# Router matmuls by depth half for both token halves, and a routing with fewer dependent VectorE steps

## The reference, cut to what matters

```python
h = rmsnorm(x, norm2_g[l]) * (1.0 + sc2) + sh2
scores = sigmoid(t @ w_router)                     # t: 256 x 1024, w_router: 1024 x 16
biased = (scores + router_bias).reshape(-1, 4, 4)
group_score = top_k(biased, 2)[0].sum(-1)
gmask = one_hot(top_k(group_score, 1))
masked = where(gmask, biased, -inf).reshape(-1, 16)
_, eidx = top_k(masked, 2)
w = sel / sel.sum(-1)                              # sel: the scores at eidx
y = sum over e of combine[:, e] * ((silu(t @ w_gate[e]) * (t @ w_up[e])) @ w_down[e])
```

## Time and profile before

| | us |
|---|---|
| median of 3 runs (1921.39, 1922.25, 1922.89) | 1922.25 |
| the profiled execution's own time | 1920.49 |
| its span, first to last instruction | 1918.9 |
| PE busy | 1844.8 (96%) |
| DVE busy | 761.5 (40%) |
| ACT busy | 660.6 (34%) |
| mean granted clock of TensorE | 0.991 |

### The profile page before, as it was taken

The page is one execution under the profiler, slowest core; times in us unless marked ns, Lnnn a source line. Parts: engine busy times, 40 slices in busy tenths (PEclk is TensorE's granted clock), DMA queues, the critical chain, the costliest instruction groups (busy, mean ns, idle before and its releaser), DMA issues.

```text
span 1918.9 us, 28438 instructions
## 1 busy us (share of the span) xinstructions
PE 1844.8 (96%) x11852; PEld 1309.1 (68%) x11852; DVE 761.5 (40%) x1285; ACT 660.6 (34%) x1064; POOL 65.3 (3%) x128
## 2 busy tenths in 40 slices
PE   5999999989999999999999999999999999899998
PEld 3888785323335888784333336676799989679998
DVE  4593553000004683652000004222455566656554
ACT  2325441111114325532111122141244546645443
POOL 0000001100001000001100010000000000000000
PEclk9999999999999999999999999999999999999999
DMA  9769865999976675865999957879954433434440
GB/s 380 299 264 383 344 244 218 426 428 427 428 305 268 246 287 220 317 263 233 427 427 427 414 202 296 353 294 418 392 201 175 175 132 118 161 139 176 175 175 22
DMA packets 52754, 540.88 MB, mean 282 GB/s; under 512 B 6768, under 2 KB 11248, under 8 KB 21680
## 3 DMA queue, kind: packets, MB, share of 16 engines
q1 hardware_dynamic: 42800, 505.66, 65.3%
q0 software_dynamic: 9856, 33.82, 4.6%
HBM read 589.53 MB, written 28.84 MB: 322 GB/s over the span
## 4 chain that ended last, share of the span: by engine, by line
PE 79%; DMA 8%; DVE 7%; DVEq 2%; issue 2%; ACT 1%; SPq 1%; POOL 0%; POOLq 0%; ACTq 0%
PE bank L1356 14%; PE bank L990 11%; PE bank L991 11%; PE bank L992 11%; PE bank L1381 6%; PE bank L1027 6%; DMA ring<-in_w_up 5%; PE bank L1036 3%; PE bank L1559 3%; PE bank L1160 2%; PE bank L1486 1%; PE bank L1507 1%; SPq L837 1%; DMA ring<-in_lru_w_out 1%; PE bank L1334 1%
## 5 line engine op out<-in xcount | busy, mean ns | idle before, releaser
L990 PE MATMUL bank<-split_x,split_w 128*128 128x256 f32 x1024 | 290.7, 284 | 2.3 <-DVE split_w L2790 2.3
L992 PE MATMUL bank<-split_x,split_w 128*128 128x256 f32 x1024 | 290.4, 284 | 0.0
L991 PE MATMUL bank<-split_x,split_w 128*128 128x256 f32 x1024 | 290.4, 284 | 0.0
L2672 DVE TENSOR_TENSOR hidden<-cqkv,bank 128x256 f32<-128x256 f32 x46 | 19.4, 421 | 515.1 <-ACT cqkv L1911 515.1
L990 PEld LDWEIGHTS bank<-split_x,split_w 128*128 128x128 f32 x1024 | 197.0, 192 | 3.3 <-DVE split_w L2790 3.3
L991 PEld LDWEIGHTS bank<-split_x,split_w 128*128 128x128 f32 x1024 | 197.1, 192 | 0.0
L992 PEld LDWEIGHTS bank<-split_x,split_w 128*128 128x128 f32 x1024 | 197.0, 192 | 0.0
L2790 DVE TENSOR_TENSOR split_w<-ring,split_w 128x1024 fp32r<-128x1024 f32 x128 | 156.3, 1225 | 92.6 <-ACT split_w L2046 92.6
L991 PE MATMUL bank<-hx_lo,ring_lo 128*128 128x256 f32 (+1 forms) x656 | 185.8, 283 | 0.0
L2046 ACT ACTIVATE split_w<-ring 128x1024 fp32r<-128x1024 f32 x128 | 133.8, 1050 | 92.1 <-PE bank L992 91.4
L990 PE MATMUL bank<-hx_hi,ring_lo 128*128 128x256 f32 (+1 forms) x528 | 152.0, 288 | 0.0
(11 more groups left out here) (407 smaller groups left out, 2849.0 us busy)
## 6 DMA issues: line engine op xcount, KB each, us to landing
ring<-in_ada SPq DMA_DIRECT2D x48, 2048.0 KB, 11.8
ring<-in_w_gate SPq DMA_DIRECT2D x32, 2048.0 KB, 13.1
ring<-in_w_up SPq DMA_DIRECT2D x32, 2048.0 KB, 18.2
ring<-in_w_down SPq DMA_DIRECT2D x32, 2048.0 KB, 16.6
ring<-in_mlp_w SPq DMA_DIRECT2D x32, 2048.0 KB, 7.7
ring<-in_w_in SPq DMA_DIRECT2D x16, 2048.0 KB, 11.7
mix<-in_w_gate SPq DMA_DIRECT2D x14, 2048.0 KB, 15.6
mix<-in_w_up SPq DMA_DIRECT2D x14, 2048.0 KB, 20.1
```

Of the source, the lines that this page charges most:

```text
L990: pe.matmul(out, hi, x_hi, start=start, stop=False, **kw)
L991: pe.matmul(out, hi, x_lo, start=False, stop=False, **kw)
L992: return pe.matmul(out, lo, x_hi, start=False, stop=stop, **kw)
```

## The change

On PE the router's loops are turned: the first depth half is multiplied for both token halves, then PE runs 4 fillers (5 before) and waits for "h2 1", then comes the second depth half for both token halves. On DVE `first_best` fuses comparison and weighting into one `scalar_tensor_tensor` per token half (two instructions with no drain between them, in place of two with one); the mask over groups is one bound and one `min` instead of a copy, a product, a bound and a sum; the masking of the first choice is one fused instruction. In `places()` the three chained comparisons of the counts become one comparison with three limits and a sum; own offsets and counts are added early; `first` is built from `below`. The fillers ahead of `picked` (13) and ahead of the one-hot matrices (21) are as before.

```diff
-        order = sb("order", NE)[:, :]
+        order_sb = sb("order", NE + 3)
+        order, limits = order_sb[:, 0:NE], order_sb[:, NE:NE + 3]
...
-                for t in range(TT):
-                    for k in range(KT):
-                        if t == 0 and k == KT // 2:
-                            keep_busy(pe, banks[7], 5)
-                            pe.wait_ge(DV.sem, DV.at("h2 1", l))
-                        ins = pe.matmul(b[:, NE * t:NE * t + NE], h_t[:, k, P * t:P * t + P],
-                                        wr[:, k, :], start=(k == 0), stop=(k == KT - 1))
+                for half in range(2):
+                    if half:
+                        keep_busy(pe, banks[7], 4)
+                        pe.wait_ge(DV.sem, DV.at("h2 1", l))
+                    for t in range(TT):
+                        for k in range(4 * half, 4 * half + 4):
+                            ins = pe.matmul(b[:, NE * t:NE * t + NE], h_t[:, k, P * t:P * t + P], wr[:, k, :],
+                                            start=(t == 0 and k == 0), stop=(k == KT - 1), skip_group_check=True)
...
-                tt(is_top, x, top.broadcast_to([P, TT, n]), ALU.is_equal)
-                wait()
-                tt(is_top, is_top, heads(order, TT), ALU.mult)
+                for t in range(TT):
+                    stt(is_top[:, t, :], x[:, t, :], top[:, t, :], order, ALU.is_equal, ALU.mult)
...
-            inside = cols(TT * NG, EG)
-            nc.vector.tensor_copy(inside, best.rearrange("p t g -> p (t g)").unsqueeze(2)
-                                  .broadcast_to([P, TT * NG, EG]))
+            bound = cols(TT, NG)
+            ts(bound, best, -2 * NEG, NEG, ALU.mult, ALU.add)
             wait()
             left = cols(TT * NG, EG)
-            out = cols(TT * NG, EG)
-            tt(left, g, inside, ALU.mult)
-            ts(out, inside, -NEG, NEG, ALU.mult, ALU.add)
-            wait()
-            tt(left, left, out, ALU.add)
-            wait()
+            tt(left, g, bound.rearrange("p t g -> p (t g)").unsqueeze(2).broadcast_to([P, TT * NG, EG]), ALU.min)
...
-            ts(out, one.rearrange("p t e -> p (t e)").rearrange("p (g e) -> p g e", e=EG), 2 * NEG, None, ALU.mult)
-            wait()
-            tt(left, left, out, ALU.add)
+            stt(flat(left), one, 2 * NEG, flat(left), ALU.mult, ALU.add)
...
-            ts(more, total, CAP + 0.5, None, ALU.is_gt)
-            wait()
-            stt(more, total, 2 * CAP + 0.5, more, ALU.is_gt, ALU.add)
-            wait()
-            stt(more, total, 3 * CAP + 0.5, more, ALU.is_gt, ALU.add)
+            tt(steps, total.unsqueeze(2).broadcast_to([P, NE, 3]), limits.unsqueeze(1).broadcast_to([P, NE, 3]), ALU.is_gt)
             wait()
+            nc.vector.tensor_reduce(more, steps, AX, ALU.add)
+            tt(base, seen, heads(const("own"), TT), ALU.add)
...
-            tt(over, over, seen, ALU.add)
-            wait()
-            tt(over, over, heads(const("own"), TT), ALU.add)
```

More of the change, by code:

```diff
@@ L2177, in routing @@
         def routing():
-            tt, ts = nc.vector.tensor_tensor, nc.vector.tensor_scalar
+            tt, ts, stt = nc.vector.tensor_tensor, nc.vector.tensor_scalar, nc.vector.scalar_tensor_tensor
             wait = nc.vector.drain
@@ L2265, in places @@
             total = counts[:, TT * NE:(TT + 1) * NE]
-            more, upto, first = line(), line(), line()
-            ts(more, total, CAP + 0.5, None, ALU.is_gt)
+            more, upto, first, below = line(), line(), line(), line()
+            over, base, steps = cols(TT, NE), cols(TT, NE), cols(NE, 3)
+            tt(steps, total.unsqueeze(2).broadcast_to([P, NE, 3]), limits.unsqueeze(1).broadcast_to([P, NE, 3]), ALU.is_gt)
             wait()
-            stt(more, total, 2 * CAP + 0.5, more, ALU.is_gt, ALU.add)
-            wait()
-            stt(more, total, 3 * CAP + 0.5, more, ALU.is_gt, ALU.add)
+            nc.vector.tensor_reduce(more, steps, AX, ALU.add)
+            tt(base, seen, heads(const("own"), TT), ALU.add)
             wait()
             nc.vector.tensor_tensor_scan(upto, ones[:, 0:NE], more, 0.0, ALU.mult, ALU.add)
+            stt(below, more, -float(CAP), const("more"), ALU.mult, ALU.add)
             wait()
-            tt(first, upto, more, ALU.subtract)
-            passed = cols(XB, NE)
+            stt(first, upto, float(CAP), below, ALU.mult, ALU.add)
+            passed = krs[:, 0:XB * NE].rearrange("p (a b) -> p a b", a=XB)
             tt(passed, upto.unsqueeze(1).broadcast_to([P, XB, NE]),
@@ L2279, in places @@
             wait()
-            stt(first, first, float(CAP), const("more"), ALU.mult, ALU.add)
+            stt(over, seen, CAP - 0.5, heads(first, TT), ALU.is_gt, ALU.mult)
             which = cols(XB, 1).rearrange("p w a -> p (w a)")
             nc.vector.tensor_reduce(which, passed, AX, ALU.add)
-            over = cols(TT, NE)
-            ts(over, seen, CAP - 0.5, None, ALU.is_gt)
             wait()
-            tt(over, over, heads(first, TT), ALU.mult)
+            tt(over, over, base, ALU.add)
             ts(extra[:, 0:XB], which, NE - 1.0, None, ALU.min)
             ts(extra[:, XB:2 * XB], which, NE - 0.5, None, ALU.is_lt)
-            wait()
-            tt(over, over, seen, ALU.add)
-            wait()
-            tt(over, over, heads(const("own"), TT), ALU.add)
             wait()
@@ L2312, in _ @@
                 nc.vector.memset(order[:, i:i + 1], float(NE - i))
+            for i in range(3):
+                nc.vector.memset(limits[:, i:i + 1], (i + 1) * CAP + 0.5)
             dve.drain().then_inc(V0.sem, V0.one("zeros"))
```

## The result

The changed kernel takes 1903.57 us (median of 6 runs, 1902.71 to 1906.05); the kernel before 1921.82 us beside it. The ratio is 0.9912, 95% interval 0.9901 to 0.9922: 16.9 us faster, where I had forecast 5.5 and a range that ended at 1914.2. The medians are 18.2 us apart; the gains in this text are those of the ratio, which is estimated over the runs and can differ from the quotient of the medians by 1 to 2 us. Every kernel was timed beside the kernel before on the same chip. The profiled execution has a span of 1902.1 us.

A forecast was written before the change was run, and what follows sets the result against it. PE holds most of the chain of waits, DVE with its queue some 9%, counting only where PE waits. Per layer 1.5 + 1.1 + 0.65 - 0.5 = 2.75 us, two layers 5.5: 1922.25 to 1916.75 us, range 1914.2 to 1919.6.

The forecast's parts named there:

- The start: Program start: three more memsets beside 16 end far ahead of PE's first matmul at 9.47 us, so they cost nothing.
- The routing's sum: Both layers' routing: 1.5 + 1.1 + 0.65 - 0.5 = 2.75 us gained a layer, 5.5 us in all.
- Router: Router on PE: turned loops leave fewer instructions at half clock, gaining 1.5 us a layer, between 0.7 and 2.3.
- rival 3: Router on PE: the clock falls earlier, at the router's start, making the kernel slower, 2.8 us a layer, 1927.8; chance 0.05.
- Choice on DVE: Choice of experts, L2193 to L2242: 5 steps fewer and 2 riders more gain 1.1 us a layer.
- rider: On DVE: an instruction without a drain ahead of it, taken to start 0.11 us behind its neighbour.
- my lower bound: Choice of experts on DVE: if each of three scalar-reading pairs cost a step after all, the gain is 0.8 us.
- Places on DVE: `places()`, L2267 to L2300: 3 steps fewer, one rider more, a wider first comparison; 0.65 us a layer, bounds 0.5 and 0.8.
- 13 fillers: PE ahead of `picked`: fillers may delay the counts 1.3 us, 0.8 remaining; loss taken as 0.5 a layer, between 0 and 1.2.
- Rival 1: Fillers ahead of `picked` become the wait: 2.75 us lost in a layer; half such loss in both gives 1919.3; chance 0.15.
- 21 fillers and the way to the end: Behind the counts: 0.2 us of waiting is left, so fillers don't hold PE; all gain passes through the experts' stage.
- rival 4: Experts' stage: nothing reaches the end because transfers set the stage from a moment of their own, 1922; chance 0.05.

The follow-up runs named there:

- the unshifted change: The changed kernel with its three limits kept in free room of `epsb`, so every tile lies where it lay before: 1915.62 us, ratio 0.9979 to the kernel before.
- the shift alone: The kernel before with only tile `order` three elements longer, so everything behind it begins 32 bytes higher: 1907.78 us, ratio 0.9928.

## Why the prediction was wrong

**The step that failed** is the sum's silent premise that nothing outside the two routings changes: two layers at 2.75 us and nothing else. "The start" counted what lengthening `order` costs in memsets, and set it at nothing; it did not ask what it moves. The shift is worth 13.8 us by itself, four fifths of the result, and I had no term, no bound and no rival for it. The addresses could have been worked out beforehand. That a split matmul would speed up with them could not: no row of before shows two distances.

**The routing's sum**, 5.5 us, measured 4.0 (2.3 to 5.8) with the tiles in place: right in kind, somewhat too large. Its terms:

- *Router.* 1.5 us a layer forecast. In the trace 2.0 us in the first layer, nothing in the second. With the clock falling as late as in my working it came out (4.84 us against 5.3); in the second layer it fell 2.0 us after the router's start, within the fillers, a moment for which I had only rival 3. In the traces of the unshifted change and of the router's loops alone it did not fall in the second layer's router at all, which then took 4.40 us, 2.1 less than before; but it fell within the counts or right behind them instead, the 21 fillers took 6.2 and 7.1 us instead of 4.7, and the gathering waited for them (7.34 and 9.00 us behind the counts' start instead of 6.93). So what the router won was in part paid back behind it, a link that my terms, added one by one, did not have. Alone, the edit gave 1.7 us (0 to 3.3) in both layers together. The case that the time depends on where the clock falls was named; that it moves by 2 us and more between layers and executions was undersized.
- *Two readings of the clock* in that term were off. A share of 0.68 over 861.0 to 861.5, with 0.50 as the low level, puts the fall at 861.18 and not at 861.34, and by the same rule the clock came back at 297.98 and not at 297.9. The second layer's 1.65 us becomes 1.5, which is what the sum used.
- *Choice on DVE.* 1.1 us a layer forecast, 0.87 in the first layer's trace (6.26 to 5.39) and 0.84 in the second's. The mis-sized price is the rider: two neighbours that read only tensors still start 0.11 us apart (295.25 and 295.36 above), but the pair that reads a per-partition scalar takes 0.46 us to the next step (292.75 to 293.21), where the two steps it replaced took 0.53. That is 0.09 us a pair more than forecast, for three pairs. The fused pairs gave next to nothing, as my lower bound had it. That the scalar operand is the reason was not tested.
- *Places on DVE.* 0.65 forecast; to the gathering 4.88 us in the first layer and, from 864.92 for L2261, 4.58 in the second, against 5.22 before: 0.34 and 0.64. The difference between the layers is one step: L2267, which has no drain ahead of it, starts 0.39 us behind its neighbour in the first layer, with 0.20 of idle time that the profile ascribes to nothing (298.80 to 299.19 above), and 0.10 behind it in the second (865.58 to 865.68).
- By the rule of the Trainium skill ("VectorE: DVE Perf Modes", "Rules for kernel authors"), which counts operations and not waits, both chains would gain 1.3 us a layer; the traces show 1.2 in the first and 1.5 in the second. Its sum is nearer than mine (1.75), though the 0.11 us between plain neighbours stands against its reason.

*13 fillers.* Forecast 1.3 us of lateness in the first layer, 0.8 of it lost; the trace shows the counts 1.4 us late and DVE idle for 0.84. PE's timeline of the unshifted version with 13 fillers, first layer, shows the same:

```profile
286.82 1.96 PE L1298 MATMUL bank<-w_router,h_t 128*128 128x16 f32 x16 [0.53 <-DVE h_t L2413]
...
291.92 3.65 PE L1305 MATMUL bank<-con,h_t 128*128 128x128 f32 x16
295.80 3.50 PE L981 MATMUL bank<-zeros 128*128 128x512 bf16 x12 [0.22 <-issue]
299.13 0.29 PE L1312 MATMUL bank<-small,con 128*128 128x16 f32 x2
...
305.24 1.02 PE L1326 MATMUL bank<-mix 128*128 128x128 f32 x7 [0.38 <-DVE mix L2645]
```

From 295.80 to 299.13 PE runs the fillers, and the counts follow without a wait. The loss that I set at 0.5 a layer was about right by the traces: DVE waited 0.84 and 0.34 us for the counts in the two layers of the changed kernel, 0.58 and nothing in the unshifted one, and nothing with 6 fillers. Rival 1, with 2.75 us lost in a layer, did not come. The runs put a higher value on the seven fillers, 4.6 and 4.0 us (about 1 to 8); what the rest of it is, and how much of it is the clock, stays open.

*21 fillers and the way to the end.* The gathering still waited 0.39 us in the first layer and not at all in the second (869.50 behind 864.73): my 0.2 us of slack was about right. The gain did pass through the experts' stage, 5.4 us earlier at its first weight load (315.14 against 320.57), and that stage itself took as long as before, so rival 4 is out.

**Why the distance matters** stays open. Shown is: what counts is where `mix`, with the moving operands, lies relative to the ring, with the stationary ones; it changes the pace of the split matmuls by steps from 116.7 to 120.0 ns. It is not only a matter of one matmul's own pair: a part of the mixers' split matmuls move `hx_lo`, which lies in `h_t` and did not move, nor did the ring, and yet from the start of such a one to the next (whose moving operand is in `mix`) it was 119.7 ns before and 117.5 in the changed kernel. It doesn't take other engines or transfers either: from 1880 to 1890 us, with no DMA at all (share 0.00), the pace is 120.0 ns before and 116.7 with `mix` alone moved, and in the MLPs' intervals with no DVE or ACT instruction within 50 ns it is 120.1 and 116.2. Plain float32 matmuls that read from `mix` were not seen to change (L1381, now L1383, 595 and 594 ns). Only times were measured, so nothing here shows the mechanism. Nor is it known why the same distance gives an MLP 179.2 us at one time and 180.9 at another, even within one execution. It is 1.7 us an MLP, less than the spread from 1902 to 1912 us in the runs of the shift alone, of which one was traced.

## What to carry to other kernels

A diff that makes a tile longer moves every tile behind it: work out the new addresses, and when a result is larger than the edit, time the shift alone before explaining the edit. To judge a small change, keep the layout (put new constants into free room). And whenever a chain gets shorter, look at the work that was put in to bridge the wait: the fillers sized for the old wait held the counts back by 1.4 us for the new one, of which 0.8 reached DVE, and taking seven out gave some 4 us more by the runs (1 to 8), of which the traces place 0.6 and 1.7 at the fillers.

## What the runs showed of the hardware that I had not expected

- A 128x256 split matmul (stationary and moving operands both in SBUF) starts every 120.0 ns at the old distance of its two operands' tiles in SBUF, every 118.7 with the moving one 128 bytes higher, 117.8 with 64, and 116.7 or 117.8 with 32, which is worth 0.7% of this kernel's time. Moving both by 32 bytes changes nothing.
- Two small VectorE instructions with no drain between them start 0.11 us apart if they read tensors; a pair of `scalar_tensor_tensor` with per-partition scalars started 0.15 us apart and held the next step back to 0.46 us, 0.2 more than one instruction.
- The moment at which the clock falls within the same work moved from 3.6 and 4.0 us after the router's start to 2.0 us in the second layer of the changed kernel. In the first layer of the version with 6 fillers, and in the second of the unshifted one with 13, it fell only at the 21 fillers, which then took 6.2 us instead of 4.7 and held the gathering.
